# Opening of a transformer block: shift and scale rows of the modulation summed together, split between VectorE and TensorE

## The reference, cut to what matters

```python
D_MODEL, SEQ, D_FF, N_MOD = 1024, 256, 2816, 9

def first_block(x, c, w_ada, b_ada, g_pre, g_post, w_ffn_gate, w_ffn_up, w_ffn_down, ...):
    mods = (jax.nn.silu(c) @ w_ada[l] + b_ada[l]).reshape(B, N_MOD, D_MODEL)
    shift = lambda i: mods[:, 3 * i]
    scale = lambda i: mods[:, 3 * i + 1]
    n = modulate(rmsnorm(h, g_pre[l, 0]), shift(0), scale(0))   # x * (1 + scale) + shift
    f = swiglu(n, w_ffn_gate[l, 0], w_ffn_up[l, 0], w_ffn_down[l, 0])
    h = h + 0.5 * gate(0) * rmsnorm(f, g_post[l, 0])
    ...
```

## Time and profile before

| | |
|---|---|
| three runs | 1116.19, 1116.29, 1117.72 us (median 1116.29) |
| profiled execution | 1115.9 us, of which its span from first to last instruction is 1114.2 us |
| busy over the span | PE 1075.0 us (96%), DVE 854.8 us (77%), ACT 549.4 us (49%) |
| mean granted TensorE clock | 0.995 |
| moved by DMA | 266.65 MB, 239 GB/s on average |

### The profile page before, as it was taken

How to read it: one execution, slowest core, us unless ns; L and a number is a source line. 1 busy time by engine, 2 the same in 40 slices (tenths; PEclk the granted TensorE clock), 3 DMA queues, 4 the chain that set the end, 5 groups by cost and what they waited for, 6 DMA issues and landing times.

```text
span 1114.2 us, 16414 instructions
## 1 busy us (share of the span) xinstructions
PE 1075.0 (96%) x6258; PEld 937.7 (84%) x6258; DVE 854.8 (77%) x924; ACT 549.4 (49%) x664; POOL 48.7 (4%) x78
## 2 busy tenths in 40 slices
PE   5799999999999999999999999999999999999997
PEld 3689999979988798888978888888888878888886
DVE  6888988678977787887878988867875787666664
ACT  4434434464675744444464444444654456444442
POOL 0000000011031100000010000001100000000001
PEclk9899999999999999999999999999999999999999
DMA  8899998636433589987569999754562446666641
GB/s 305 311 387 400 396 385 291 196 120 228 151 114 120 182 309 322 312 304 251 194 242 332 344 363 343 251 186 132 176 203 100 161 142 218 223 214 229 210 170 57
DMA packets 147045, 266.65 MB, mean 239 GB/s; under 512 B 9673, under 2 KB 104246, under 8 KB 141750
## 3 DMA queue, kind: packets, MB, share of 16 engines
q1 hardware_dynamic: 145104, 262.69, 67.9%
q0 software_dynamic: 1056, 3.17, 0.8%
q10 hardware_dynamic: 838, 0.15, 0.1%
HBM read 263.34 MB, written 2.65 MB: 239 GB/s over the span
## 4 chain that ended last, share of the span: by engine, by line
PE 87%; DVE 5%; ACT 3%; DMA 2%; issue 1%; SPq 1%; POOL 1%; POOLq 0%; DVEq 0%; ACTq 0%
PE ps L1879 16%; PE ps L1813 12%; PE ps L1815 12%; PE ps L1814 12%; PE ps L1881 8%; PE ps L1860 7%; PE ps L1863 7%; PE ps L1862 7%; DMA w_raw<-in_w_ffn_up 1%; DVE arena L1391 1%; DMA arena<-in_w_ada 1%; DVE w_lo L1154 1%; ACT w_hi L785 1%; ACT nT_both L785 1%; PE ps L2313 1%
## 5 line engine op out<-in xcount | busy, mean ns | idle before, releaser
L1154 DVE TENSOR_TENSOR w_lo<-w_raw,w_hi 128x2048 fp32r<-128x2048 f32 (+2 forms) x170 | 382.7, 2256 | 116.6 <-ACT w_hi L785 115.5
L785 ACT ACTIVATE w_hi<-w_raw 128x2048 fp32r<-128x2048 f32 (+2 forms) x170 | 319.4, 1884 | 264.1 <-PE ps L1815 111.6
L1879 PE MATMUL ps<-nT_both,w_hi 128*128 128x512 f32 x768 | 272.0, 398 | 0.0
L1881 PE MATMUL ps<-nT_both,w_lo 128*128 128x256 f32 x768 | 215.6, 281 | 0.0
L1860 PE MATMUL ps<-nT_both,w_hi 128*128 128x256 f32 x672 | 191.3, 285 | 1.4 <-DVE h_act L1267 1.4
L1863 PE MATMUL ps<-nT_both,w_lo 128*128 128x256 f32 x672 | 190.1, 283 | 0.0
L1862 PE MATMUL ps<-nT_both,w_hi 128*128 128x256 f32 x672 | 190.1, 283 | 0.0
L1879 PEld LDWEIGHTS ps<-nT_both,w_hi 128*128 128x128 f32 x768 | 144.3, 188 | 35.7
L1881 PEld LDWEIGHTS ps<-nT_both,w_lo 128*128 128x128 f32 x768 | 145.0, 189 | 0.9
L1860 PEld LDWEIGHTS ps<-nT_both,w_hi 128*128 128x128 f32 x672 | 128.8, 192 | 2.7 <-DVE h_act L1267 1.9
L1235 DVE SCALAR_TENSOR_TENSOR arena<-arena,c_act 128x3072 f32<-128x3072 f32 (+2 forms) x49 | 129.3, 2651 | 1.4 <-DMA arena<-in_ada_w 1.4
(11 more groups left out here) (277 smaller groups left out, 1204.7 us busy)
## 6 DMA issues: line engine op xcount, KB each, us to landing
arena<-in_w_ada SPq DMA_DIRECT2D x16, 1536.0 KB, 10.3
arena<-in_ada_w SPq DMA_DIRECT2D x16, 1536.0 KB, 8.4
w_raw<-in_w_ffn_down SPq DMA_DIRECT2D x44, 512.0 KB, 4.8
w_raw<-in_w_in SPq DMA_DIRECT2D x44, 512.0 KB, 4.5
w_raw<-in_ffn_w_down SPq DMA_DIRECT2D x44, 512.0 KB, 4.1
w_raw<-in_w_ffn_gate SPq DMA_DIRECT2D x42, 512.0 KB, 6.9
w_raw<-in_w_ffn_up SPq DMA_DIRECT2D x42, 512.0 KB, 8.0
w_raw<-in_ffn_w_gate SPq DMA_DIRECT2D x42, 512.0 KB, 4.2
```

Of the source, the lines that this page charges most:

```text
L785: copy = lambda o, i: act.activation(o, i, ACT.Copy)
L1154: dve.tensor_tensor(lo(s, n), raw(s, n), hi(s, n).bitcast(F32), ALU.subtract).then_inc(lo_ready[s], 1)
L1879: pe.matmul(ps[:, i, :], hi(s)[:, cols], nT_both[:, kk].rearrange("p a n -> p (a n)"), start=(kk == 0), stop=False, skip_group_check=True)
L1881: last = pe.matmul(ps[:, i, 0:S], lo(s)[:, cols], nT_hi[:, kk, :], start=False, stop=(kk == KD - 1), skip_group_check=True)
```

## The change

Each row `j` now comes with its shift and its scale columns together: one transfer of 512 KB per row and half, 16 in all, of the same bytes as before. Within half 0 DVE sums rows 0 to 5 and PE rows 6 and 7; within half 1 DVE sums rows 0 to 4 and PE rows 5 to 7. DVE's operations are 1024 columns wide. PE sums a row by eight products with a 128x128 piece of the row as the weights that it loads and one column of `c_act` as what streams through. DVE has one fold per half and takes the outcome out in two steps: `first_folded` (four operations of 32 partitions) and `first_out` (one that adds PE's rows, one with the gain). SP's loads stand in another order: chunk 2's first half of gate weights is issued right after chunk 1's, and in chunk 1 of `ffn_loads` the second half of chunk 2's gate weights stands between the two `ada` transfers.

```diff
-        FIRST = [(m, half, q) for half in range(2) for m in range(2) for q in range(2)]
+        ON_DVE = [range(0, 6), range(0, 5)]
+        ON_PE = [range(6, KD), range(5, KD)]
...
                 if f == "F0":
-                    sp.wait_ge(first_sum, KD)
+                    sp.wait_ge(first_sum, sums_to[2])
+                    sp.wait_ge(fold_mm, FOLDS.index("rows 1") + 1)
...
-                chunk(1)
+                if f == "F0":
+                    load_down(f, 0)
+                    load_ada(f, 0, 0)
+                    load_gu(f, 1, 2)
+                    load_ada(f, 1, 0)
+                else:
+                    chunk(1)
...
-            for i in range(2):
-                load_first(i)
+            for j in range(4):
+                load_first(0, j)
...
             load_gu("F0", 0, 0)
-            load_first(4)
+            for j in ON_PE[0]:
+                load_first(0, j)
+            sp.wait_ge(first_sum, 2)
+            for j in range(2):
+                load_first(1, j)
             load_gu("F0", 0, 1)
-            for i in range(5, KD):
-                load_first(i)
+            for j in range(2, 6):
+                sp.wait_ge(first_sum, j + 1)
+                load_first(1, j)
             load_gu("F0", 1, 0)
-            sp.wait_ge(first_sum, 6)
+            sp.wait_ge(fold_mm, FOLDS.index("rows 0") + 1)
+            for j in range(6, KD):
+                load_first(1, j)
+            sp.wait_ge(first_sum, sums_to[1] + 2)
             load_gu("F0", 1, 1)
+            load_gu("F0", 0, 2)
...
+            first_rows(0, ON_DVE[0])
+            first_fold(0)
             vectors()
             dve.wait_ge(vec_ready, 2)
-            first_out(0, 0)
-            first_out(1, 0)
+            first_folded(0)
             split_lo(*gate_up("F0", 0, 0))
+            first_out(0)
             norm_lo("F0", 0, 0)
+            first_rows(1, range(1))
...
+            first_rows(1, ON_DVE[1][2:])
+            first_fold(1)
             split_lo(*gate_up("F0", 1, 0))
+            first_folded(1)
+            first_out(1)
...
+            def first_rows_sum(half):
+
+                for j in ON_PE[half]:
+                    pe.wait_ge(first_loaded[j], 16 * (half + 1))
+                    for k in range(KD):
+                        last = pe.matmul(ps[:, fold_bank(f"rows {half}"), k:k + 1], first_at[half][j][:, k * P:(k + 1) * P],
+                                         c_act[:, 0, j:j + 1], start=(j == ON_PE[half][0] and k == 0), stop=(j == ON_PE[half][-1]),
+                                         skip_group_check=True)
+                last.then_inc(fold_mm, 1)
...
                     if half == 0:
-                        gate_up_half("F0", 0, 1)
-                        first_fold(0, 1)
-                        first_fold(1, 1)
+                        gate_up_half("F0", 0, 1, mid=lambda: first_rows_sum(1))
+                        first_fold(1)
```

More of the change, by code:

```diff
@@ L120, in program @@
         first_acc = carve(4608, 2, NB)
-        first_raw = carve(2 * ADA, 3, 2 * D)
-        first_at = [first_raw[:, 0], first_raw[:, 1], first_raw[:, 2], gate[:].rearrange("p a n -> p (a n)"),
-                    first_raw[:, 0], w_raw[:, SLOT_B], first_raw[:, 1], first_raw[:, 2]]
-        first_free = {4: 1, 6: 2, 7: 4}
+        first_raw = carve(2 * ADA, 6, D)
+        slots = [first_raw[:, i] for i in range(6)] + [gate[:, i, :] for i in range(2)] + \
+                [w_raw[:, SLOT_B, i * D:(i + 1) * D] for i in range(2)]
+        first_at = [slots[0:8], slots[8:10] + slots[0:6]]
         pick = carve(18688, P)
@@ L276, in program @@
         }
-        FOLDS = ["shift 0", "scale 0", "shift 1", "scale 1", "F0", "F0 late", "F1", "F2", "F2 late", "F3"]
+        FOLDS = ["first 0", "rows 0", "rows 1", "first 1", "F0", "F0 late", "F1", "F2", "F2 late", "F3"]
         fold_cols = {
@@ L1396, in first_fold, with first_rows @@
-            def first_fold(m, half):
-                dve.wait_ge(first_sum, 4 * half + 2 * m + 2)
-                dve.tensor_reduce(folds[:, 2 * half + m, 0:16], first_acc[:, m, :].rearrange("p (r q) -> p r q", q=Q), AX.X, ALU.add,
+            first_sums = first_acc.rearrange("p m n -> p (m n)")
+            def first_rows(half, js):
+                for j in js:
+                    dve.wait_ge(first_loaded[j], 16 * (half + 1))
+                    row, c = first_at[half][j], c_act[:, 0, j:j + 1]
+                    if j == 0:
+                        dve.tensor_scalar(first_sums, row, c, None, ALU.mult).then_inc(first_sum, 1)
+                        continue
+                    dve.wait_ge(first_sum, sums_to[half] + j)
+                    dve.scalar_tensor_tensor(first_sums, row, c, first_sums, ALU.mult, ALU.add).then_inc(first_sum, 1)
@@ L1400, in first_fold, with first_folded @@
+            def first_fold(half):
+                dve.wait_ge(first_sum, sums_to[half + 1])
+                dve.tensor_reduce(folds[:, half, :], first_sums.rearrange("p (r q) -> p r q", q=Q), AX.X, ALU.add,
                                   apply_transpose=True).then_inc(folded, 1)
-            def first_out(m, half):
-                group = f"{('shift', 'scale')[m]} {half}"
+            def first_folded(half):
+                k = slice(4 * half, 4 * half + 4)
+                group = f"first {half}"
@@ L1405, in first_out @@
                 dve.wait_ge(fold_mm, FOLDS.index(group) + 1)
[L1406 removed]
                 for g in range(P // Q):
                     rows = slice(g * Q, (g + 1) * Q)
[L1409 to L1410 removed]
+                    last = dve.tensor_tensor(mod_col[rows, 0, 1::-1, k],
+                                             ps[rows, fold_bank(group), g:Q:P // Q].rearrange("p (m k) -> p m k", k=4),
+                                             vec_col[rows, 0, 0:2 * KD].rearrange("p (m k) -> p m k", k=KD)[:, :, k], ALU.add)
@@ L1966, in sum_folds @@
             def sum_folds(f):
[L1968 removed]
+                pe.wait_ge(folded, folded_to(f))
                 n = len(fold_cols.get(f, []))
@@ L1975, in sum_folds, with first_fold @@
                 last.then_inc(fold_mm, 1)
-            def first_fold(m, half):
-                i = 2 * half + m
-                pe.wait_ge(folded, i + 1)
-                pe.matmul(ps[:, fold_bank(FOLDS[i]), 0:16], pick, folds[:, i, 0:16], start=True, stop=True).then_inc(fold_mm, 1)
+            def first_fold(half):
+                group = f"first {half}"
+                pe.wait_ge(folded, folded_to(group))
+                pe.matmul(ps[:, fold_bank(group), 0:Q], pick, folds[:, half, :], start=True, stop=True).then_inc(fold_mm, 1)
+            def first_rows_sum(half):
[6 more added lines that the diff above has]
+                last.then_inc(fold_mm, 1)
             def opening():
```

76 lines of the change are left out of this document (22 added, 54 removed).

## The result

| | median, us | runs | profiled execution | its span |
|---|---|---|---|---|
| before | 1116.29 | 1116.19 to 1117.72 (5) | 1115.90 | 1114.2 |
| after | 1124.27 | 1121.48 to 1125.55 (5) | 1125.55 | 1123.8 |

The ratio is 1.0066, 95% interval 1.005 to 1.0082: the change makes the kernel slower by 0.66%. The direction was predicted, the size was not: 1119.6 was forecast, and 1124.27 lies 0.7 us above the top of the range (1123.6).

A forecast was written before the change was run, and what follows sets the result against it. PE, busy 96% of the span, was the bound, with chunk 2's start passing on one to one: `first_mods` 2 4.9 us later, chunk 2 3.3 later; 1115.9 + 3.3 = 1119.2, median 0.4 above, 1119.6 us; range 1115.6 to 1123.6.

The forecast's parts named there:

- What bounds the kernel: PE is busy 96% of the span; a shift in chunk 2's start, 71.14 us before, passes on one to one.
- The price of a one-column product: PE's row sums: 0.44 us per one-column product at the lower clock, 0.22 at the full one.
- Rival (c): A one-column product costs half the price, 0.22 us at the lower and 0.11 at the full clock; 1113.4 us; chance 0.08.
- Half 0: PE's rows end at 30.1 us, first large product at 32.3 against 29.39, 2.9 us later.
- (a): Rival: the clock falls during half 1's 24 one-column products, moving `first_mods` 2 by 2.8 us; 1122.4 us; chance 0.27.
- (b): Rival: one-column products keep or raise the clock, half 0's rows end at 28.4; 1117.2 us; chance 0.22.
- my case: The main forecast: chunk 2 starts 3.3 us later, at 74.4; 1119.6 us; chance 0.38.
- Half 1 up to `first_mods` 2: PE's queue, 19.1 us from first large product to the small one, sets `first_mods` 2 at 52.5, before 47.63.
- PE issues without a pause: The argument against the clock falling during half 1's 24 one-column products.
- From `first_mods` 2 to chunk 2: SP's loads wait for a split, `ada` lands at 69.6, DVE's steps follow; chunk 2 at 74.4 us, 21.9 after `first_mods` 2.
- M + 8.9 for the split: ACT's 4.7 and 1.9 us and DVE's 2.3 put the split of chunk 1's second weights at 61.4.
- five units back to back at 3.26 us: Units of 1 MB, timed from 49.92 to 66.22 before; 2.5 of them behind the split were to take 8.2 us.

The follow-up runs named there:

- a2_after_again: The changed kernel run and profiled a second time with no edit; 1122.72 us, ratio 1.0067 to the kernel before.
- f1_narrow_fill: Fourteen idle one-column products added behind half 1's small product, in PE's pause, to `e5_wide_dve`; 1112.95 us, ratio 0.9972 to the kernel before.
- e1_ada_first: The changed kernel with the second `ada` transfer ahead of chunk 2's second gate weights in SP's queue; 1119.05 us, ratio 1.0025 to the kernel before.
- e3_dve_half0: The changed kernel with all eight rows of half 0 summed on DVE, half 1 still split five to three; 1125.79 us, ratio 1.0084 to the kernel before.
- e2_spread: The changed kernel with half 1's 24 one-column products spread, two ahead of each three 256-column products; 1119.97 us, ratio 1.0038 to the kernel before.
- e9_out_first: `e3_dve_half0` with half 0's gain written ahead of the split of chunk 0's weights; 1123.16 us, ratio 1.007 to the kernel before.
- e5_wide_dve: The changed kernel with all rows on DVE, rows 6 and 7 loaded earlier, gain ahead of the split, second `ada` ahead; 1111.48 us, ratio 0.9963 to before.

## Why the prediction was right and wrong

*What bounds the kernel.* Right: the start of chunk 2 passes on to the end one to one. Behind it nothing moved in nine of the twelve other profiles; in two the clock was down at chunk 2's start, and in one a microsecond is untraced.

*The price of a one-column product.* Right. I took 0.44 us at the lower clock and 0.22 at the full one; measured 6.83 / 16 = 0.43 and 5.86 / 24 = 0.24. Rival (c), half of that, is out. The two passes of weights are paid in full however few the columns. With that the Trainium skill (TensorE: Matmul & The Clock Gate, LDWEIGHTS), whose formula, columns over 1.2 GHz, makes no difference between the levels of the clock and gives 107 ns for 128 columns, is contradicted a second time: 0.21 us a pass at the lower clock.

*Half 0.* Right for the profiled execution: PE's rows ended at 30.25 (forecast 30.1), the first large product was at 32.53 (32.3). But it is no constant. I took the lower clock for granted because the spacing in the one profile of before said so; `a2_after_again` has the full clock in the same place and is 2.6 us earlier. The executions of the changed kernel differ there by as much as rivals (a) and (b) differ from my case.

*Half 1 up to `first_mods` 2.* Here the main step failed. Forecast: chunk 1's first 24 products at 40.1, the one-column products to 48.3, the other 24 at 0.12 each to 51.2, M at 52.5. Measured: 40.7, 49.3, 54.5, and M at 56.1. Of the 3.6 us, 1.0 had gathered by 49.3 and 2.3 are the second 24 products at the lower clock (5.2 us instead of 2.9); the small product and the steps behind it make the rest. It is rival (a), to which I gave 0.27 and 2.8 us. The step that failed is that PE keeps its full clock through the 24 one-column products: it fell after 4.8 us of them (43.55 to 48.4). My argument against it, "PE issues without a pause", was the mistake: `f1_narrow_fill` shows that issuing without a pause is not what counts. I had the counterpart in hand, a fall between 46 and 50, and read it as the effect of a pause alone.

*From `first_mods` 2 to chunk 2.* With M the moment of `first_mods` 2, M + 8.9 for the split held (64.97 with M at 56.1). The landing did not: I had 8.2 us behind the split, from five units back to back at 3.26 us, and it was 9.9 (65.0 to 74.9). The stretches around the two starts, after and, below, before:

```profile
64.00:66.00 2.00, 2.00 (x13) 1.74 (x13) 1.49 (x3) 0.60 (x2) 0.00 (x0) 1.00 0.00 0
66.00:68.00 2.00, 2.00 (x19) 2.00 (x18) 0.56 (x2) 1.58 (x1) 0.00 (x0) 1.00 0.82 228
```
```profile
50.00:52.00 2.00, 1.69 (x4) 1.44 (x5) 0.95 (x3) 1.94 (x7) 0.00 (x0) 0.50 0.49 150
52.00:54.00 2.00, 2.00 (x6) 1.54 (x6) 0.43 (x1) 2.00 (x2) 0.00 (x0) 0.50 1.06 408
```

In both kernels the queue had run dry and started late, here about 1.9 us behind the issue at 65.00, before about 1.3 behind the one at 49.92 (estimates, from the bytes of these stretches and a flow of 400 to 420 GB/s). My 3.26 us per unit holds such a start already, but spread over five units, and I took only half of them: that alone is 0.7 of the 1.7 us, and the start was longer by 0.6. What the last 0.4 are is not shown; some 3.3 MB moved up to 74.9, where the two pieces are 2.6, so later loads shared the queue. From the landing to PE the forecast was 4.8, measured 4.7. So chunk 2 is late by 3.6 and 1.7, less 0.1: 79.58 against 74.4.

*What was missing.* The clock at chunk 2's start. PE had rested 2.56 us, and the clock fell in it and stayed down for some 3 us behind (products 0.21 us apart up to 82.5): 1.1 us more, which no case of mine had. The wait that the change was to take away had come back as one of 2.56 us, and it cost more than its length. In `e1_ada_first` the wait goes and the clock stays up. But a wait here doesn't always bring the clock down: it fell in the 2.56 us of this profile and the 3.30 of `e3_dve_half0`, and not in the 1.53 of `a2_after_again`, the 2.32 of `e2_spread` and the 3.08 of `e9_out_first`. What decides it no run shows.

In sum: 1119.2 + 3.6 + 1.7 - 0.1 + 1.1 = 1125.5, the time of the profiled execution. The median is 1.3 below it; the second profile, 4.2 us shorter, had half 0's products at the full clock and no fall at chunk 2, and how often either happens is not known. The range failed because I let (a) stand alone: together with the two smaller errors of the same sign, the landing and the clock at chunk 2, it lies outside.

*Where the gain went.* VectorE did get quicker as forecast, and the early gate weights were worth 1.5 us. Both were lost to the products on PE, for which `first_mods` 1 and 2 waited (DVE idled 4.4 us for PE in half 0 and 8.1 in half 1 of the profile after), and to the second `ada` transfer behind the wait for `lo_ready1`. With these products left out, the same layout and the early gate weights are worth 4.3 us, together with earlier loads of rows 6 and 7, the gain ahead of the split and the second `ada` transfer ahead (`e5_wide_dve`).

## What to carry to other kernels

A matrix-vector product on TensorE costs its loading of weights however narrow it is; before moving sums to it, count the passes, never put them ahead of what everybody waits for, and spread them between wide products. A queue that has nothing left to send starts again late, so when a load sits behind a wait count the start by itself and not as a part of a mean rate per megabyte. And when a step leaves the critical path, look at what stands next to it in the same engine's queue: twice here a split of 2.3 us took the place of what had been removed.

## What the runs showed of the hardware

- One-column float32 products one behind the other do not hold TensorE's clock. In half 1 it fell after 3.6 us of them in `a2_after_again`, 4.3 in `e1_ada_first` and 4.8 in the changed kernel, read from stretches of 1 us, with PE busy all the time; spread among 256-column products (`e2_spread`) they did no harm, and fourteen 128-column products held the clock where fourteen one-column ones of the same length did not.
- A one-column float32 product takes 0.24 us at the full clock and 0.43 at the lower one, as much as one of 128 columns at the full clock (3.37 us for fourteen of 128 columns, 3.27 for fourteen of one).
- At one place of one kernel the clock can be at either level from one execution to the next: 6.83 and 4.13 us for the same sixteen products. What decides it I could not show; one difference ahead of the place is that in the slow one PE's transposes were broken off for 0.96 us (to 20.48), in the fast one they ran through. The column of the granted clock names 1.00 for the slow one of the two, so there the spacing of the products is the better witness.
- A dry DMA queue starts late: nothing moved in 64 to 66 us behind an issue at 65.00 (0 GB/s), and the flow began about 1.9 us behind the issue; in the kernel before it was about 1.3 us behind the one at 49.92 (estimates as above).
